# Two-layer hybrid backbone on one core: token statistics in a three-column form, and four weight units run k by k behind each pre-norm

## The reference, cut to what matters

```python
def rmsnorm(x, g):
    y = x * lax.rsqrt(jnp.mean(x * x, axis=-1, keepdims=True) + RMS_EPS)
    return y * g

h = rmsnorm(x, g[0]) * (1 + m[0, 1]) + m[0, 0]                       # sub-block 0: ffn_a, D_FF = 2816
x = x + 0.5 * m[0, 2] * rmsnorm(swiglu(h, wg[0], wu[0], wd[0]), g[1])
h = rmsnorm(x, g[2]) * (1 + m[1, 1]) + m[1, 0]                       # sub-block 1: Fourier | Hyena | attention
x = x + m[1, 2] * rmsnorm(mix(h @ w_in) @ w_out, g[3])
h = rmsnorm(x, g[4]) * (1 + m[2, 1]) + m[2, 0]                       # sub-block 2: ffn_b
x = x + 0.5 * m[2, 2] * rmsnorm(swiglu(h, wg[1], wu[1], wd[1]), g[5])
```

## Time and profile before

| | before |
|---|---|
| median of 3 executions | 1689.71 us |
| the profiled execution | 1690.58 us |
| its span, first to last instruction | 1688.4 us |
| TensorE matmul busy | 1590.5 us (94%) |
| VectorE busy | 897.8 us (53%) |
| ScalarE busy | 662.7 us (39%) |
| mean granted TensorE clock | 0.984 |
| DMA | 260.29 MB, mean 154 GB/s |

### The profile page before, as it was taken

How to read it: one execution, slowest core, us unless ns; L and a number is a source line. 1 busy time by engine, 2 the same in 40 slices (tenths; PEclk the granted TensorE clock), 3 DMA queues, 4 the chain that set the end, 5 groups by cost and what they waited for, 6 DMA issues and landing times.

```text
span 1688.4 us, 22839 instructions
## 1 busy us (share of the span) xinstructions
PE 1590.5 (94%) x9302; PEld 1453.2 (86%) x9302; DVE 897.8 (53%) x1591; ACT 662.7 (39%) x1096; POOL 17.8 (1%) x39
## 2 busy tenths in 40 slices
PE   6899999998988899999989999999898889999996
PEld 2399989996966699989979998999697569999996
DVE  5655545336685665544336554433657656555433
ACT  2334333335525544433334433333453554444332
POOL 0000000000000000000000000000010000000000
PEclk9999999999999899999999999999999999999998
DMA  6833675345500433384352367544450053333431
GB/s 243 328 112 123 248 297 188 122 171 179 187 1 32 168 125 125 125 299 137 129 184 97 122 227 296 210 134 165 164 188 28 13 187 113 125 125 122 137 128 64
DMA packets 68051, 260.29 MB, mean 154 GB/s; under 512 B 8843, under 2 KB 9900, under 8 KB 67308
## 3 DMA queue, kind: packets, MB, share of 16 engines
q1 hardware_dynamic: 64572, 240.49, 40.4%
q0 software_dynamic: 3376, 18.35, 2.9%
HBM read 252.26 MB, written 6.55 MB: 153 GB/s over the span
## 4 chain that ended last, share of the span: by engine, by line
PE 87%; DVE 8%; ACT 2%; issue 1%; DMA 1%; SPq 0%; ACTq 0%; DVEq 0%
PE bank L511 26%; PE bank L513 25%; PE bank L512 25%; PE bank L520 3%; PE bank L849 1%; PE bank L811 1%; DMA w_m<-w_mod 1%; DVE rstd L1245 1%; PE bank L735 1%; DVE y L1250 1%; PE bank L599 1%; DVE sb_s L1436 1%; PE bank L572 1%; ACT prob_t L1050 1%; DVE x L1252 1%
## 5 line engine op out<-in xcount | busy, mean ns | idle before, releaser
L1186 DVE TENSOR_TENSOR w_lo<-w_raw,w_hi 128x1024 fp32r<-128x1024 f32 (+2 forms) x288 | 373.5, 1297 | 528.7 <-ACT w_hi L909 527.8
L511 PE MATMUL bank<-h_hi,w_hi 128*128 128x386 f32 (+1 forms) x1760 | 605.1, 344 | 0.6 <-DVE w_lo L1186 0.6
L513 PE MATMUL bank<-h_hi,w_lo 128*128 128x386 f32 (+1 forms) x1760 | 596.4, 339 | 0.0
L512 PE MATMUL bank<-h_lo,w_hi 128*128 128x386 f32 (+1 forms) x1760 | 595.9, 339 | 0.0
L909 ACT ACTIVATE w_hi<-w_raw 128x1024 fp32r<-128x1024 f32 (+2 forms) x288 | 322.5, 1120 | 583.3 <-PE bank L513 583.1
L511 PEld LDWEIGHTS bank<-h_hi,w_hi 128*128 128x128 f32 x1760 | 332.2, 189 | 16.7 <-issue 12.7
L512 PEld LDWEIGHTS bank<-h_lo,w_hi 128*128 128x128 f32 x1760 | 332.9, 189 | 1.2
L513 PEld LDWEIGHTS bank<-h_hi,w_lo 128*128 128x128 f32 x1760 | 332.4, 189 | 0.0
L513 PE MATMUL bank<-hid_hi,w_lo 128*128 128x384 f32 x704 | 236.6, 336 | 0.0
L512 PE MATMUL bank<-hid_lo,w_hi 128*128 128x384 f32 x704 | 236.6, 336 | 0.0
L511 PE MATMUL bank<-hid_hi,w_hi 128*128 128x384 f32 x704 | 236.5, 336 | 0.0
(11 more groups left out here) (192 smaller groups left out, 1024.1 us busy)
## 6 DMA issues: line engine op xcount, KB each, us to landing
w_raw<-w_gu SPq DMA_DIRECT2D x176, 512.0 KB, 3.4
w_m<-w_mod SPq DMA_DIRECT2D x144, 512.0 KB, 6.5
w_raw<-w_dn SPq DMA_DIRECT2D x64, 704.0 KB, 4.0
w_raw<-w_in SPq DMA_DIRECT2D x26, 512.0 KB, 3.6
w_raw<-w_out SPq DMA_DIRECT2D x16, 512.0 KB, 3.4
...
```

Of the source, the lines that this page charges most:

```text
L511: mm(out, w_hi[:, wn, c], rhs_hi, start=first, stop=False)
L512: mm(out, w_hi[:, wn, c], rhs_lo, start=False, stop=False)
L513: return mm(out, w_lo[s][:, c], rhs_hi, start=False, stop=last)
L1186: TT(w_lo[unit % RAW][:, 0:n], w_raw[unit % RAW][:, 0:n], w_hi[:, unit % HIS, 0:n], ALU.subtract).then_inc(unit_lo.sem, 1)
```

## The change

- **Statistics in three columns.** The roles of the operands are turned round: the squares (128 features x 128 tokens) are the stationary operand and one column of `ones` the moving one. The mean of squares of 128 tokens then lies on 128 partitions in one column, and of 384 tokens in 128 x 3. The root and the reciprocal work on 128 x 3. Three matmuls with `ident` as the moving operand (`widen`) spread the reciprocals again to 128 x 384 in a PSUM bank.
- **Post-norm.** `sums` on `ss` and on the eighth tile's squares (three matmuls each), root, reciprocal, `widen`; VectorE multiplies `y` by the bank directly. It goes through k in chunks of 1, 1, 2, 2, 2.
- **Pre-norm.** ScalarE makes `h_hi` ahead of the squares of a chunk. VectorE no longer adds squares. TensorE sums them with 24 one-column matmuls, six each in four places: after k = 3, 5 and 6, and after the second unit's last k.
- **Four units k by k.** `first_units` now runs four units in four banks, for each k all four (12 matmuls), and no longer one after the other. The first half of the job's rows stands ahead of them and the second half behind them and behind `widen`.
- **Slots and order.** `HIS` goes from 2 to 4, and the high and low parts of a unit are made one unit earlier, up to three units ahead of a norm; the fourth unit's are made inside the norm. The norm between the layers is run like the others. Tiny activations load the tables of Sqrt and Silu ahead of their use. Banks are freed by `gate_scaled`, `up_scaled` and `in_scaled`. `fa`, `sb_s2` and `stat` of the mixers move to other addresses, `g_lat` moves within the constants, and one initial constant DMA replaces two.

The core of the diff:

```diff
-HIS = 2
+HIS = 4
+CHUNKS = ((0, 1), (1, 2), (2, 4), (4, 6), (6, 8))
+NCH = len(CHUNKS)
+TT3 = T // P
...
-            def pre_norm(layer, n, tiles=None):
+            def norm_rows(layer, n, part):
                 landed = layer * (32 * JL) + (JOB_NORM[n] * 32 + 64)
-                pe.wait_ge(mod_copied.sem, mod_copied.at(layer, JOB_NORM[n]))
-                job_rows(landed, range(MSLOT))
-                for c in range(4):
-                    if n:
-                        pe.wait_ge(xsq_added.sem, xsq_added.at(layer, 4 * n + c - 3))
-                        last = mm(bank[STAT][:, 0:T], ones[:, :], sq[:, c % 2, :], start=c == 0, stop=c == 3)
-                    else:
-                        pe.wait_ge(xsq_done.sem, xsq_done.at(layer, c + 1))
-                        for k in range(2):
-                            last = mm(bank[STAT][:, 0:T], ones[:, :], xsq[:, c % 2, k, :], start=c == 0 and k == 0,
-                                      stop=c == 3 and k == 1)
-                    last.then_inc(xsq_used.sem, 1)
-                    if c == (ROWS_AT if n else 3):
-                        job_rows(landed, range(MSLOT, KT))
-                    if tiles:
-                        tiles(c)
-            def first_units(layer, n, base, banks, c):
-                def one(u, k):
-                    last = three(bank[banks[u]][:, 0:TB], (base + u) % RAW, (base + u) % HIS, k, h_hi[:, k, :],
-                                 h_lo[:, k, :], k == 0, k == KT - 1)
-                    if k == KT - 1:
-                        last.then_inc(units_done.sem, 1)
-                if c == 0:
-                    pe.wait_ge(unit_lo.sem, unit_lo.at(layer, base + 1))
-                if c == 3:
-                    pe.wait_ge(unit_lo.sem, unit_lo.at(layer, base + 2))
-                    for k in range(2):
-                        one(1, k)
-                for k in (2 * c, 2 * c + 1):
+                if not part:
+                    pe.wait_ge(mod_copied.sem, mod_copied.at(layer, JOB_NORM[n]))
+                job_rows(landed, range(MSLOT, KT) if part else range(MSLOT))
+            def sums(col, src, first, last):
+                for t in range(TT3):
+                    m = mm(bank[STAT][:, col + t:col + t + 1], src[:, t * P:(t + 1) * P], ones[:, 0:1],
+                           start=first and t == 0, stop=last and t == TT3 - 1)
+                return m
+            def widen(out, col):
+                for t in range(TT3):
+                    m = mm(bank[out][:, t * P:(t + 1) * P], rs[:, col, t:t + 1].broadcast_to([P, P]), ident[:, :],
+                           start=t == 0, stop=t == TT3 - 1)
+                return m
+            def pre_sum(layer, n, c):
+                pe.wait_ge(xsq_done.sem, xsq_done.at(layer, 4 * n + c + 1))
+                sums(S_ROW, xsq[:, c % 2, 0, :], c == 0, False)
+                sums(S_ROW, xsq[:, c % 2, 1, :], False, c == 3).then_inc(xsq_used.sem, 1)
+            def first_units(layer, n, base, banks):
+                norm_rows(layer, n, 0)
+                for k in range(KT):
                     pe.wait_ge(nlo_done.sem, nlo_done.at(layer, KT * n + k + 1))
-                    one(0, k)
-                if c == 3:
-                    for k in range(2, KT):
-                        one(1, k)
+                    for u in range(4):
+                        if k == 0:
+                            pe.wait_ge(unit_lo.sem, unit_lo.at(layer, base + u + 1))
+                        last = three(bank[banks[u]][:, 0:TB], (base + u) % RAW, (base + u) % HIS, k, h_hi[:, k, :],
+                                     h_lo[:, k, :], k == 0, k == KT - 1)
+                        if k == KT - 1:
+                            last.then_inc(units_done.sem, 1)
+                            if u == 1:
+                                pre_sum(layer, n, 3)
+                    if k % 2 and 3 <= k < KT - 1 or k == KT - 2:
+                        pre_sum(layer, n, (k - 3) // 2 if k % 2 else 2)
+                pe.wait_ge(pre_inv.sem, pre_inv.at(layer, n + 1))
+                widen(PRE, 1).then_inc(pre_wide.sem, 1)
+                norm_rows(layer, n, 1)
...
-                mm(bank[STAT][:, 0:T], ones[:, :], ss[:, :], start=True, stop=False)
+                sums(P_ROW, ss, True, False)
                 pe.wait_ge(out_sq.sem, out_sq.at(layer, KT * n + KT))
-                mm(bank[STAT][:, 0:T], ones[:, :], sq[:, (KT - 1) % 2, :], start=False,
-                   stop=True).then_inc(ss_add.sem, 1)
+                sums(P_ROW, sq[:, (KT - 1) % 2, :], False, True).then_inc(ss_add.sem, 1)
+                pe.wait_ge(out_taken.sem, out_taken.at(layer, KT * n + KT - 1))
+                pe.wait_ge(post_inv.sem, post_inv.at(layer, n + 1))
+                widen(POST, 0).then_inc(post_wide.sem, 1)
...
+                        free = up_scaled if up else gate_scaled
+                        pe.wait_ge(free.sem, free.at(layer, tile - 1))
+                        pe.wait_ge(unit_lo.sem, unit_lo.at(layer, unit + 1))
...
+                if layer or n:
+                    pe.wait_ge(up_scaled.sem, up_scaled.at(layer, FT * n))
+                first_units(layer, 2 * n, B_GU[n], (GATE[0], UP[0], GATE[1], UP[1]))
...
-            def pre_norm(layer, n):
+            def pre_norm(layer, n, base):
                 act.wait_ge(coef_ready.sem, coef_ready.at(layer, 2 * n))
                 A(h_hi[:, :, T:TB], coef_b[:, :, :], ACT.Copy)
-                if not n:
-                    hi_part(layer, 0)
-                for c in range(4):
-                    act.wait_ge(x_new.sem, x_new.at(layer, 4 * (n - 1) + c + 1))
-                    if n:
-                        act.wait_ge(xsq_added.sem, xsq_added.at(layer, 4 * n + c - 5))
-                    else:
-                        act.wait_ge(xsq_used.sem, xsq_used.at(layer, c - 1))
-                    A(xsq[:, c % 2, :, :], x[:, 2 * c:2 * c + 2, :], ACT.Square).then_inc(xsq_done.sem, 1)
-                    for k in (2 * c, 2 * c + 1):
+                for i, (a, b) in enumerate(CHUNKS):
+                    if layer or n:
+                        act.wait_ge(x_new.sem, x_new.at(layer, NCH * (n - 1) + i + 1))
+                    for k in range(a, b):
                         for s, cols in enumerate((CTX, LAT)):
                             last = A(h_hi[:, k, cols], x[:, k, cols], ACT.Copy, scale=coef_a[:, k, s:s + 1])
                         last.then_inc(nhi_done.sem, 1)
-                if not n:
-                    hi_part(layer, 1)
+                    if i:
+                        c = i - 1
+                        if c >= 2:
+                            act.wait_ge(xsq_used.sem, xsq_used.at(layer, 4 * n + c - 1))
+                        A(xsq[:, c % 2, :, :], x[:, 2 * c:2 * c + 2, :], ACT.Square).then_inc(xsq_done.sem, 1)
+                    if i == 1:
+                        hi_part(layer, base + 3)
                 act.wait_ge(xsq_used.sem, xsq_used.at(layer, 4 * n + 4))
-                A(sd[:, :], bank[STAT][:, 0:T], ACT.Sqrt, bias=epsc[:, :]).then_inc(pre_sd.sem, 1)
+                A(sd[:, 1, 0:TT3], bank[STAT][:, S_ROW:S_ROW + TT3], ACT.Sqrt,
+                  bias=epsc[:, :]).then_inc(pre_sd.sem, 1)
+                if n != 1:
+                    A(junk[:, 4:5], epsc[:, :], ACT.Silu)
...
-                A(sd[:, :], bank[STAT][:, 0:T], ACT.Sqrt, bias=epsc[:, :]).then_inc(post_sd.sem, 1)
+                A(sd[:, 0, 0:TT3], bank[STAT][:, P_ROW:P_ROW + TT3], ACT.Sqrt,
+                  bias=epsc[:, :]).then_inc(post_sd.sem, 1)
...
+                A(junk[:, 0:1], epsc[:, :], ACT.Sqrt)
                 act.wait_ge(coef_ready.sem, coef_ready.at(layer, 4 * n + 1))
                 for t in range(KT):
-                    for u in (2 * t + 2, 2 * t + 3):
-                        if B_DN[n] + u < UNITS:
-                            hi_part(layer, B_DN[n] + u)
+                    for u in (2 * t + 3, 2 * t + 4):
...
-            def input_lo(layer, n, c):
-                if c == 0:
+            def input_lo(layer, n, i, base):
+                if i == 0:
                     dve.wait_ge(coef_ready.sem, coef_ready.at(layer, 2 * n))
-                if n:
-                    dve.wait_ge(xsq_done.sem, xsq_done.at(layer, 4 * n + c + 1))
-                    dve.wait_ge(xsq_used.sem, xsq_used.at(layer, 4 * n + c - 1))
-                    TT(sq[:, c % 2, :], xsq[:, c % 2, 0, :], xsq[:, c % 2, 1, :], ALU.add).then_inc(xsq_added.sem, 1)
-                for k in (2 * c, 2 * c + 1):
+                for k in range(*CHUNKS[i]):
                     dve.wait_ge(nhi_done.sem, nhi_done.at(layer, KT * n + k + 1))
                     if k == 0:
                         TT(h_lo[:, :, T:TB], coef_b[:, :, :], h_hi[:, :, T:TB], ALU.subtract)
...
                         last = STT(out=h_lo[:, k, cols], in0=x[:, k, cols], scalar=coef_a[:, k, s:s + 1],
                                    in1=h_hi[:, k, cols], op0=ALU.mult, op1=ALU.subtract)
```

(43 more changed lines are left out.)

275 lines of the change are left out of this document (133 added, 142 removed).

## The result

The changed kernel takes 1697.05 us, median of six executions (1691.86 to 1704.66); six of the kernel before beside them gave a median of 1688.75 (1687.20 to 1690.12). The ratio is 1.0054, with a 95% interval of 1.0031 to 1.0076: slower by 8.3 us, where 8.5 us of gain was forecast. The time lies inside the range given; the direction is wrong. The profiled execution took 1697.58 us, its span 1695.7, against 1690.58 and 1688.4 before.

The account below looks back on a forecast made before the run. TensorE was taken as the bound, with savings counting only where it stands still, chiefly the norm pairs. Pairs, contention (+0.6), start (+0.5) and end (-2.6) summed to -8.5 us: 1682.1 profiled, forecast 1681.2, range 1667 to 1701.

Parts of the forecast that it names:

- The lead: First norm pair, from the last down matmul (zero): first `y` product at 2.95 us against 6.83 before, k = 0 at 6.0.
- The price s: Time of one load-and-matmul pair with one moving column: taken as 0.111 us, entering the time 288 times.
- cheap and dear columns: Rivals on a one-column pair's price: cheap, near 0.058 us, 1666 (chance 0.10); dear, 0.15 to 0.19, 1708 at 0.192 (0.16).
- The fourth unit: First norm pair: its low part ends at 9.7 us after zero, so TensorE waits 2.1 us from 7.6.
- The run and the fifth unit: Four units k by k end the first unit at 27.5 us after zero; the fifth, behind its load, starts 6.25 later, at 33.75.
- `D`: Mark in a norm pair where the first unit is done and its slot frees for the fifth unit's load: predicted 27.5 us.
- the +0.3 of contention: Pairs one and four: four unit loads meet four GpSimd pieces that used to come one to a unit, +0.3 us each.
- the rival of late slots: Loads issued together with GpSimd pieces land late; fifth unit 3.9 us later in pairs one and four: 1689 us, chance 0.15.
- The other edits cost nothing: the earlier high and low parts: Earlier parts, `HIS = 4`, bank waits and junk activations lie under TensorE's units (VectorE 53%, ScalarE 39% busy): no cost.
- The end: Lone post-norm at the kernel's end: `y` starts 2.95 us after zero against 5.82, single chunks cost 0.27 more: -2.6 us.
- The start: From the first rows to the fifth unit: 24 one-column matmuls replace 16 pairs partly in waits, fifth unit at 102.9: +0.5 us.
- the rival of the clock: In the norm pairs TensorE stays at 1.2 GHz until some 11 us: 2 us in five places, 1691 us, chance 0.17.

Follow-up runs that it names:

- e10_double: Changed kernel with every pre-norm square counted twice, 48 one-column matmuls in place of 24 (wrong scale): 1761.64 us, ratio 1.0422.
- e13_double_64: The kernel with 48 pre-norm sums, each square counted twice, with 64 moving columns in each sum in place of one: 1726.59 us, ratio 1.0230.
- e5_wide: Changed kernel with 32 columns of ones in place of one in all sums, pre-norm and post-norm: 1694.54 us, ratio 1.0031.
- e14_64: Changed kernel with 64 columns of ones in place of one in each pre-norm sum: 1694.51 us, ratio 1.0033.
- e2_add: Changed kernel with VectorE adding the two squares of a chunk, so 12 instead of 24 one-column matmuls in each pre-norm: 1679.44 us, ratio 0.9951.
- e7_tail_add: Changed kernel with project_in's last high and low parts behind the mixers' work and VectorE adding squares (12 one-column matmuls): 1672.11 us, ratio 0.9900.
- e1_tail: Changed kernel with project_in's last high and low parts put behind what the mixers need: 1690.91 us, ratio 1.0013.

## Why the prediction was right or wrong

- **The lead** was right. In the first pair the first `y` product starts 3.17 after zero (predicted 2.95) and k = 0 at 6.17 (6.0).
- **The price s** was right. A group of twelve takes 1.26 from its first matmul to the next k's (410.17 to 411.43): 0.105 each, against 0.111. Both rivals about it, cheap and dear columns, are out. The row that I leaned on, L797, has 128 moving columns and not a short moving side; the reasoning by the load's length is what held.
- **The fourth unit** was right: a wait of 1.79 (2.1), over at 9.8 (9.7).
- **The run and the fifth unit** were right where the clock is full: `D` at 27.7 (27.5), the fifth unit 6.4 behind it (6.25). The fourth pair has the GpSimd pieces and is no longer than the second, so the +0.3 of contention isn't seen, nor the rival of late slots. They weren't tested apart.
- **The clock within the run** was wrong, in two steps. The first: I let TensorE fall only behind waits, priced that rival at 2 us a pair, and held against it that before only a wait of 6.64 had brought a fall (I also read the return of the clock there as 5 us behind the restart; it is 4.0, from 393.05 to 397.1). Falls came behind waits of at most 1.8, in four pairs of five, and cost 1.6, 0.3, 0.3 and 1.4 us. That is this rival, come true for 3.6 of the 10 us that I gave it. The second, which I didn't see, is that the matmuls I added are themselves a cause: a group of 1.26 us with twelve moving columns in it. The step that failed is 36 pairs of one column ahead of `D`, and twelve behind it, counted at their length and nothing more. The second falls cost 1.3, 1.4 and 1.3 us in three pairs. e10_double against e13_double_64 shows the cause where there are 48 of these matmuls, and with 24 it is that no pair of four units has a second fall once the sums are widened (e5_wide, e14_64) or halved in number (e2_add, e7_tail_add). That it also made the executions scatter over 13 us, where the kernel before has 3, is likely by the 3 to 4 of the wide sums, but not tested apart.
- **"The other edits cost nothing: the earlier high and low parts"** was wrong, by 7.1 us. e1_tail took 6.1 us off. I took the average busy share of ScalarE and VectorE (39%, 53%) for cover. At the tail of project_in the parts wait for a load, and the engines in order keep the last convolution, `vg_tok` and the last scaling behind them. The terms would have come out of one question at that place: is the data there, and who is queued behind?
- **The end** was right: -2.4 against -2.6. **The start** was +1.3 against +0.5. The clock was at half until 79.6, before the first sum, and `D` came at 97.0 (96.7 predicted); the other 0.5 lies behind `D`, with the fifth unit 6.7 after it (6.25).

Forecast and result, in the profiled executions: 1682.1, plus 8.5 for the pairs (-6.4 forecast, +2.1 measured), 7.1 mixers, 0.8 start, 0.4 project_out, 0.2 end, less 1.2 elsewhere, gives 1697.9, against 1697.58. Of the 8.5, second falls are 4.0 and first falls 3.6; the rest is small sizes. A chance of 0.21 for slower was too low for the reason above: the rival that I called the slower side has a cause that isn't there, the rival of the clock came true in part, and neither the tail nor the second falls were among them. That the time lies in the range says little, since the range was wide enough to hold the kernel before too. Open is what decides in which execution and pair the first fall comes (it is missing in the fourth pair of the profiled execution, and e1_tail, with the same code in the pairs, has it at other places).
